# Block 1's feed-forwards: seven block products instead of eight for each pair of up slices, with one weight sum of four made by an accumulating DMA

## What is computed

```python
for l in range(DEPTH):                       # DEPTH = 2
    h = _swiglu(x, ffn_w1[l, 0], ffn_w3[l, 0], ffn_w2[l, 0])
    x = _layernorm(ALPHA * x + 0.5 * h, ln_g[l, 0], ln_b[l, 0])
    h = _mixer(x, l, ...)
    x = _layernorm(ALPHA * x + h, ln_g[l, 1], ln_b[l, 1])
    h = _swiglu(x, ffn_w1[l, 1], ffn_w3[l, 1], ffn_w2[l, 1])
    x = _layernorm(ALPHA * x + 0.5 * h, ln_g[l, 2], ln_b[l, 2])
```

## Time and profile before

| | us |
|---|---|
| median of 3 runs | 1950.27 (1950.02 to 1951.34) |
| the profiled execution's own time | 1950.56 |
| its span | 1948.7 |
| granted TensorE clock, mean | 0.999 |
| TensorE busy | 1919.6 |
| VectorE busy | 1196.0 |
| ScalarE busy | 924.4 |

### The profile page before, as it was taken

How to read it: one execution, slowest core, us unless ns; L and a number is a source line. 1 busy time by engine, 2 the same in 40 slices (tenths; PEclk the granted TensorE clock), 3 DMA queues, 4 the chain that set the end, 5 groups by cost and what they waited for, 6 DMA issues and landing times.

```text
span 1948.7 us, 24336 instructions
## 1 busy us (share of the span) xinstructions
PE 1919.6 (99%) x9160; PEld 1576.5 (81%) x9160; DVE 1196.0 (61%) x1471; ACT 924.4 (47%) x1147; POOL 101.2 (5%) x168
## 2 busy tenths in 40 slices
PE   9999999999999999999999999989999999999999
PEld 7888888888888788888888888877788887778887
DVE  5555866677445645577667655578755466775545
ACT  5443445545443543443554534357644355654443
POOL 2000100000000100010000000011000000100000
PEclk9999999999999999999999999999999999999999
DMA  9675554546655765565354765465365545346542
GB/s 318 196 226 194 200 191 148 173 152 194 215 189 177 219 227 194 173 224 186 131 172 151 225 206 179 148 173 184 128 234 172 172 170 186 119 147 215 179 165 87
DMA packets 202155, 357.69 MB, mean 184 GB/s; under 512 B 8048, under 2 KB 101152, under 8 KB 201824
## 3 DMA queue, kind: packets, MB, share of 16 engines
q1 hardware_dynamic: 195856, 334.85, 51.5%
q0 software_dynamic: 6224, 21.82, 3.9%
HBM read 353.49 MB, written 1.05 MB: 182 GB/s over the span
## 4 chain that ended last, share of the span: by engine, by line
PE 92%; DVE 5%; DVEq 1%; ACT 1%; issue 0%; DMA 0%; SPq 0%
PE acc L717 52%; PE aux L717 32%; DVE w_low L2160 2%; PE aux L833 2%; PE aux L732 1%; PE aux L987 1%; DVE xT_low L2166 0%; DVE x_res L2248 0%; DMA w_raw<-ffn_w 0%; PE aux L997 0%; PE aux L1033 0%; PE aux L996 0%; PE aux L1011 0%; DVE buf_k L2945 0%; DVE x_res L2241 0%
## 5 line engine op out<-in xcount | busy, mean ns | idle before, releaser
L2160 DVE TENSOR_TENSOR w_low<-w_raw,w_high 128x2048 fp32r<-128x2048 f32 (+1 forms) x304 | 686.6, 2271 | 417.3 <-ACT w_high L1589 415.1
L1589 ACT CAST w_high<-w_raw 128x2048 fp32r<-128x2048 f32 (+1 forms) x312 | 586.7, 1896 | 432.3 <-PE acc L717 324.6
L717 PE MATMUL aux<-w_high,xT_high 128*128 128x512 f32 x960 | 380.6, 396 | 3.7 <-DVE xT_low L2166 1.7
L717 PE MATMUL aux<-w_high,xT_low 128*128 128x512 f32 x960 | 374.6, 390 | 0.0
L717 PE MATMUL aux<-w_low,xT_high 128*128 128x512 f32 x960 | 373.9, 389 | 0.0
L717 PE MATMUL acc<-w_high,yT_high 128*128 128x512 f32 (+1 forms) x836 | 329.5, 394 | 0.4 <-issue 0.4
L717 PE MATMUL acc<-w_high,yT_low 128*128 128x512 f32 (+1 forms) x836 | 325.3, 389 | 0.0
L717 PE MATMUL acc<-w_low,yT_high 128*128 128x512 f32 (+1 forms) x836 | 324.8, 388 | 0.0
L717 PE MATMUL acc<-w_high,xT_high 128*128 128x512 f32 (+2 forms) x752 | 297.6, 396 | 5.2 <-DVE xT_low L2166 4.1
L717 PE MATMUL acc<-w_high,xT_low 128*128 128x512 f32 (+2 forms) x752 | 291.3, 387 | 0.0
L717 PE MATMUL acc<-w_low,xT_high 128*128 128x512 f32 (+2 forms) x752 | 291.1, 387 | 0.0
(11 more groups left out here) (343 smaller groups left out, 1351.5 us busy)
## 6 DMA issues: line engine op xcount, KB each, us to landing
w_raw<-ffn_w SPq DMA_DIRECT2D x174, 512.0 KB
w_raw<-w_ff SPq DMA_DIRECT2D x64, 1024.0 KB
w_raw<-w_in SPq DMA_DIRECT2D x52, 1024.0 KB
w_raw<-ffn_w SPq DMA_DIRECT2D x44, 1024.0 KB
w_raw<-w_branch SPq DMA_DIRECT2D x16, 1024.0 KB
w_raw<-o_w_in SPq DMA_DIRECT2D x12, 1024.0 KB
w_raw<-w_ple_gate SPq DMA_DIRECT2D x8, 1024.0 KB
w_raw<-e_w_in SPq DMA_DIRECT2D x6, 1024.0 KB
```

Of the source, the lines that this page charges most:

```text
L717: last = nc.tensor.matmul(dst, lhs[:, kt, tok], rhs(j), start=(kt == k_first and q == 0), stop=(kt == k_last and q == 2))
L1589: nc.scalar.copy(whi[:, s, 0:size], raw[:, s, 0:size]).then_inc(slot_hi[s], 1)
L2160: V.tensor_tensor(wlo[:, s, 0:size], raw[:, s, 0:size], cast(whi[:, s, 0:size]), ALU.subtract)\
```

## The change

Of the 11 slices, 0, 1, 4, 7 and 10 stay as they were ("plain"). The others form three pairs, slices 3q+2 and 3q+3 for q = 0, 1, 2. A pair's up product is X (tiles x halves of k) times W (halves of k x [w1 | w3], 512 columns each), a 2 x 2 product of blocks, done with seven block products instead of eight:

- Four raw blocks are loaded into `buf_v`, `buf_q`, `buf_u` and `buf_val`: R11 and R21 (w1, upper and lower half of k), R12 and R22 (w3).
- VectorE adds in place: R11 + R12, then + R22, then + R21. An accumulating DMA on POOL's queue adds R22 to R12. Products b11, b21, v, x, w, y, b22 use R11, R21, the three sums in R11, the sum in R12, and R22. Each is split into high and low in the ring of slots, so a pair has seven high and seven low halves where its two slices had four of each.
- Four combinations of x (`form`) are made by VectorE once for each feed-forward and split into high and low.
- Terms are copied out of PSUM by ScalarE between products (`term1` to `term3`) and combined by VectorE.

A round is a pair and the plain slice 3q+4. A unit's place in the ring now comes from a table (`ffn_units`). The last slice's down unit has no accumulating DMA any more. The halved first unit of slice 1 goes, as do the halved units at the end; the position angles move to the start of the first feed-forward; the loops over slices are written out. The diff, cut to its core:

```diff
+QUADS = 3
+PLAIN = (0, 1, 4, 7, 10)
+FORMS = 4
...
+def quad_and_plain(q, a, b):
+    o = 3 * q + 4
+    units = [(f"b11_{q}", a), (f"b21_{q}", b), (f"v_{q}", 1), (f"x_{q}", 2), (f"d{o - 3}", a), (f"w_{q}", b),
+ (f"y_{q}", 1), (f"b22_{q}", 2), (f"h{o}_0", b), (f"h{o}_1", a), (f"d{o - 2}", 1), (f"d{o - 1}", 2)]
+    done = [f"b11_{q}", f"b21_{q}", f"v_{q}", f"x_{q}", f"w_{q}", f"d{o - 3}", f"y_{q}", f"b22_{q}",
+f"h{o}_0", f"d{o - 2}", f"d{o - 1}"]
+    return units, done
...
+def quad_load(l, which, q, r):
+    freed = {R11: "y", R21: "y", R12: "w", R22: "b22"}[r]
+    if q > 0:
+        s, n = ffn_unit(l, which, f"{freed}_{q - 1}")
+        sp.wait_ge(slot_lo[s], n + 2)
+    elif which == 1:
+        sp.wait_ge(small_free, l + 1)
+    elif l > 0:
+        sp.wait_ge(quad_free, 2 * l)
+    w = a["ffn_w1" if r in (R11, R21) else "ffn_w3"]
+    r0 = (l * 2 + which) * D + (4 * P if r in (R21, R22) else 0)
+    sp.dma_start(sum_raw[r].rearrange("p (k n) -> p k n", k=4),
+                 rows(w, r0, 4 * P, (3 * q + 2) * FB, 2 * FB)).then_inc(r_full[r], 16)
...
+    hidden1(l, which, 1, 0)
+    hidden1(l, which, 1, 1)
+    quad_load(l, which, 0, R11)
+    down1(l, which, 0)
+    for r in (R12, R21, R22):
+        quad_load(l, which, 0, r)
+    for q in range(QUADS):
+        o = 3 * q + 4
+        down1(l, which, o - 3)
+        hidden1(l, which, o, 0)
+        down1(l, which, o - 2)
+        down1(l, which, o - 1)
+        hidden1(l, which, o, 1)
+        if q + 1 < QUADS:
+            for r in (R12, R21, R11, R22):
+                quad_load(l, which, q + 1, r)
+    down1(l, which, NF - 1)
...
-def last_down_low(l, which):
-    n = 2 * l + which
-    src = raw[:, 3, :]
-    if which == 1:
-        src = rows(a["ffn_w2"], n * F1 + (NF - 1) * FB, FB, 0, D)
-    dst = wlo[:, 3, :] if which == 0 else wlo[:, 3, :].rearrange("p (k n) -> p k n", k=2)
-    pool.wait_ge(last_neg, n + 1)
-    pool.dma_start(dst, src, accum_op=ALU.add).then_inc(last_sum, 16)
-    pool.wait_ge(last_sum, 16 * n + 16)
-    pool.sem_inc(slot_lo[3], 1)
+def sums_by_dma(l, which):
+    for q in range(QUADS):
+        n = quads_before(l, which, q)
+        pool.wait_ge(sum_done, 3 * n + 1)
+        pool.wait_ge(r_full[R22], 16 * n + 16)
+        pool.dma_start(sum_raw[R12], sum_raw[R22], accum_op=ALU.add).then_inc(w_sum, 16)
...
+    def quad_product(name, q, b, lh, ll, first):
+        s = lo_wait(f"{name}_{q}")
+        for k in range(4):
+            for n, (lhs, rhs) in enumerate(((lh, whi), (lh, wlo), (ll, whi))):
+                last = nc.tensor.matmul(aux[:, b, :], lhs(k), rhs[:, s, k * NC:(k + 1) * NC],
+                                        start=(first and k == 0 and n == 0), stop=(k == 3 and n == 2), skip_group_check=not first)
+        last.then_inc(unit_used, 1)
...
+    def quad1(q):
+        o = 3 * q + 4
+        terms, combined = 5 * quads_before(l, which, q), 3 * quads_before(l, which, q)
+        pe.wait_ge(aux_read[1], aux0[1] + q + 3)
+        quad_product("b11", q, 1, *x_part(0, 0), True)
+        pe.wait_ge(aux_read[0], aux0[0] + q + 3)
+        quad_product("b21", q, 0, *x_part(0, 1), True)
+        pe.wait_ge(aux_read[3], aux0[3] + q + 1)
+        quad_product("v", q, 3, *form(0), True)
+        pe.wait_ge(quad_act, terms + 1)
+        quad_product("x", q, 1, *form(1), False)
+        plain_down(o - 3, 0)
+        pe.wait_ge(quad_act, terms + 2)
+        quad_product("w", q, 1, *form(2), False)
+        plain_down(o - 3, 1).then_inc(unit_used, 1)
+        pe.wait_ge(quad_act, terms + 3)
+        quad_product("y", q, 1, *x_part(1, 1), False)
+        pe.wait_ge(quad_read, combined + 2)
+        quad_product("b22", q, 3, *form(3), False)
...
+    hidden_unit(0, 0, 0)
+    hidden_unit(0, 0, 1, mid=lambda: x_T(l, 2 * which, 1, [0]))
+    x_T(l, 2 * which, 1, [1])
+    aux0[2:] = [n_aux[2].k, n_aux[3].k]
+    hidden(0, 1)
+    for j in range(2):
+        hidden_unit(1, 0, j)
+        if j == 1:
+            plain_T(0)
+        hidden_unit(1, 1, j)
+    for p in range(2):
+        pe.wait_ge(acc_read[p], n_acc[p].k + 1)
+    plain_down(0, 0)
+    plain_down(0, 1).then_inc(unit_used, 1)
+    plain_T(1)
+    for q in range(QUADS):
+        o = 3 * q + 4
+        quad1(q)
+        if q + 1 == QUADS:
+            break
+        hidden(o, 0)
+        quad_T(q)
+        hidden(o, 1)
+        for t in range(NT):
+            last = quad_down(o - 2, t)
+        last.then_inc(unit_used, 1)
+        plain_T(o)
+        for t in range(NT):
+            last = quad_down(o - 1, t)
+        last.then_inc(unit_used, 1)
+    i = NF - 1
+    hidden(i, 0)
+    quad_T(QUADS - 1)
+    hidden_unit(i, 1, 0)
+    quad_down(i - 2, 0)
+    quad_down(i - 1, 0)
+    last_T(0)
+    pe.wait_ge(aux_read[2], aux0[2] + FFN_AUX[2] + 1)
+    down_part(i, 0).then_inc(acc_full[0], 1)
+    hidden_unit(i, 1, 1)
+    quad_down(i - 2, 1).then_inc(unit_used, 1)
+    quad_down(i - 1, 1, [0])
...
+    tile1()
+    aux0[2:] = [n_aux[2].k, n_aux[3].k]
+    activate(0, 0)
+    high_plain("h1_0")
+    high_plain("d0")
+    activate(0, 1)
+    high_plain("h1_1")
+    loaded(0, R11)
+    high_sum("b11", 0, R11)
+    for n in range(FORMS):
+        act.wait_ge(form_done, FORMS * (2 * l + which) + (1, 3, 2, 4)[n])
+        nc.scalar.copy(form_h[:, n, :, :].rearrange("p k c -> p (k c)"), quarter[FORM_AT[n]])\
+            .then_inc(form_hi, 1)
+    if mid is not None:
+        mid()
+    used("h1_0")
+    loaded(0, R21)
+    high_sum("b21", 0, R21)
+    activate(1, 0)
+    plain_high_T(0)
+    activate(1, 1)
+    summed(0, 1)
+    high_sum("v", 0, R11)
+    used("d0")
+    plain_high_T(1)
+    summed(0, 2)
+    high_sum("x", 0, R11)
+    for q in range(QUADS):
+        o = 3 * q + 4
+        if q == 0:
+            act.wait_ge(form_lo, FORMS * (2 * l + which) + FORMS)
+        else:
+            act.wait_ge(h_ready, 2 * quads_before(l, which, q))
+        used(f"b11_{q}")
+        nc.scalar.copy(term1, aux[:, 1, :]).then_inc(quad_act, 1)
+        high_plain(f"d{o - 3}")
+        used(f"b21_{q}")
+        act.wait_ge(w_sum, 16 * quads_before(l, which, q) + 16)
+        high_sum("w", q, R12)
+        summed(q, 3)
+        used(f"v_{q}")
+        high_sum("y", q, R11)
+        used(f"x_{q}")
+        nc.scalar.copy(term2, aux[:, 1, :]).then_inc(quad_act, 1)
+        loaded(q, R22)
+        high_sum("b22", q, R22)
+        used(f"w_{q}")
+        nc.scalar.copy(term3, aux[:, 1, :]).then_inc(quad_act, 1)
+        high_plain(f"h{o}_0")
+        act.wait_ge(quad_read, 3 * quads_before(l, which, q) + 1)
+        nc.scalar.activation(term1, term1, ACT.Silu).then_inc(quad_act, 1)
+        used(f"d{o - 3}")
+        high_plain(f"h{o}_1")
+        used(f"y_{q}")
+        nc.scalar.activation(silu1, aux[:, 1, :], ACT.Silu).then_inc(quad_act, 1)
+        high_plain(f"d{o - 2}")
+        used(f"b22_{q}")
+        high_plain(f"d{o - 1}")
+        activate(o, 0)
+        quad_high_T(q)
+        used(f"h{o}_0")
+        if q + 1 == QUADS:
+            break
+        loaded(q + 1, R11)
+        high_sum("b11", q + 1, R11)
+        activate(o, 1)
+        loaded(q + 1, R21)
+        high_sum("b21", q + 1, R21)
+        used(f"d{o - 2}")
+        summed(q + 1, 1)
+        high_sum("v", q + 1, R11)
+        plain_high_T(o)
+        used(f"d{o - 1}")
+        summed(q + 1, 2)
+        high_sum("x", q + 1, R11)
+    high_plain("d10")
...
+    tile1()
+    dve.drain()
+    h0 = n_hi.k
+    whole(1, 0, 0)
+    whole(1, 1, 1)
+    multiply(0, 0)
+    whole(0, 0, 2)
+    low_plain("h1_0")
+    whole(0, 1, 3)
+    dve.drain()
+    combine(1, 0, 1, ALU.subtract)
+    dve.drain()
+    combine(0, 2, 0, ALU.subtract)
+    multiply(0, 1)
+    combine(2, 1, 2, ALU.subtract)
+    dve.drain()
+    combine(3, 3, 2, ALU.add)
+    low_plain("h1_1")
+    low_plain("d0")
+    low_sum("b11", 0, R11)
+    for n in range(FORMS):
+        form_low(n)
+    if mid is not None:
+        mid()
+    add_to(0, R11, R12)
+    low_sum("b21", 0, R21)
+    dve.wait_ge(aux_full[2], n_aux[2].k + 1)
+    multiply(1, 0)
+    plain_low_T(0)
+    multiply(1, 1)
+    for q in range(QUADS):
+        o = 3 * q + 4
+        combined, terms = 3 * quads_before(l, which, q), 5 * quads_before(l, which, q)
+        low_sum("v", q, R11)
+        plain_low_T(1 if q == 0 else o - 3)
+        add_to(q, R11, R22)
+        low_sum("x", q, R11)
+        low_plain(f"d{o - 3}")
+        add_to(q, R11, R21)
+        low_sum("w", q, R12)
+        low_sum("y", q, R11)
+        low_sum("b22", q, R22)
+        dve.wait_ge(quad_act, terms + 1)
+        dve.wait_ge(unit_used, ffn_done(l, which, f"b21_{q}"))
+        V.tensor_tensor(term1, aux[:, 0, :], term1, ALU.add).then_inc(quad_read, 1)
+        dve.wait_ge(quad_act, terms + 3)
+        V.tensor_tensor(term3, aux[:, 3, :], term3, ALU.subtract).then_inc(quad_read, 1)
+        low_plain(f"h{o}_0")
+        low_plain(f"h{o}_1")
+        dve.wait_ge(quad_act, terms + 5)
+        dve.wait_ge(quad_read, combined + 2)
```

(91 more changed lines are left out.)

431 lines of the change are left out of this document (240 added, 191 removed).

## The result

The changed kernel takes 1981.64 us (median of 4 runs, 1981.46 to 1983.09), the kernel before beside it 1950.44: a ratio of 1.016, with an interval of 1.014 to 1.018. It is 31 us slower where 24 were forecast. The profiled execution of the changed kernel took 1983.09 us with a span of 1981.1, 32.4 more than the span of before.

A forecast was written before the change was run, and what follows sets the result against it. TensorE's matmuls were taken to bound the kernel. Net of 32.7 us saved, feed-forwards (9.0 + 2.1 + 2.1 + 1.4), handovers (3.0 + 0.8) and clock (5.6) added 23.9 to 1950.56; by the median 1974 us, range 1958 to 1992.

The forecast's parts named there:

- What goes: Up products of the pairs in four feed-forwards: one block product of 12 matmuls fewer per pair, 32.7 us less.
- Costs by durations: Operation times taken from trace rows; a weight sum in place on VectorE taken as 2.29 us, bounds 2.2 and 2.5.
- Rounds two and three: Later pair rounds of each feed-forward: 47.7 us each on TensorE without a wait, 1.0 us to spare at w.
- Rival 2: Rounds stall too: accumulating DMA taking 18 us costs 2.6 in each later round, giving 1995; slower handoffs 1978; chance 0.12.
- The first down slice: Feed-forward start: TensorE waits for the low half of slice 0's transposed activations, 6.3 us, 11.0 in the first.
- Small terms: Shorter TensorE stalls: slice 1's units 1.1 and 0.4, w of the first pair 1.4, the end 1.1, handovers 1.5 twice and 0.8.
- the end: Last down slice: tile 0's last transposes are followed at once by the product that needs them, 1.1 us per feed-forward.
- the clock: Behind the long stall of each feed-forward the granted clock falls to half: 4 x 1.4 = 5.6 us, bounds 0 and twice the row.
- Rival 1: The clock does not fall in the stalls at the feed-forwards' starts: 1969 us; chance 0.13.
- the first load: First feed-forward: first down slice lands at 26.0 behind as many bytes as before; its later high half costs 2.3 us.
- Rival 3: The feed-forward start does not hold TensorE up: 1939 us; chance 0.08, with what lies between it and no change.
- Rival 4: Whole kernel: the matmuls fall away and the stalls about equal them, 1950 us; chance 0.05.

The follow-up runs named there:

- experiment 7: Changed kernel with the sum R12 + R22 made by VectorE right after low x instead of by the accumulating DMA: 2001.38 us, ratio 1.0265.
- Experiment 6: Changed kernel with three small reorderings (second-term copy ahead of high y, last transposes earlier, slot 1's low half split at handovers): 1975.49 us, ratio 1.0126.
- Experiment 5: Changed kernel with the load of slice 0's down unit issued ahead of raw block R11: 1979.11 us, ratio 1.0148.
- experiment 1: Changed kernel with VectorE's multiply and low half of slice 0's transposes right after low b11, ahead of the combined x: 1958.72 us, ratio 1.0043.
- eighth kernel: Changed kernel with transposes' low half earlier, position angles later, down load before R11, three small reorderings, two form halves in VectorE's gap: 1940.21 us, ratio 0.9943.
- ninth kernel: The eighth kernel plus high b21 after the second activation, low w before the third sum, slice 1's first unit split in halves: 1930.57 us, ratio 0.9897.

## Why the prediction was right, and where it was off

- **What goes**: 144 instructions fewer, 12 in each of 12 pairs. Held.
- **Costs by durations**: a sum in place took 2285 ns (predicted 2.29).
- **Rounds two and three**: no long wait; from the transposes of slice 4 to those of slice 7 in the second feed-forward 47.6 us (552.08 to 599.69), predicted 47.7. The count to w with 1.0 to spare stood at 1.2 in experiment 7. Rival 2 fell.
- **The first down slice**, the largest term: 6.3 predicted in each of three feed-forwards, 6.12, 6.08 and 6.11 measured. The low half begins 24.0 us behind the start of tile 1 of slice 0, predicted 23.9 (458.11 to 482.0). In the first, 11.0 predicted and 8.57 measured; TensorE had been held up 3 us more before it, and by the slow clock, and so arrived later.
- **Small terms**: first unit of slice 1 1.1, measured 1.1 (in the third feed-forward 0.55); second unit 0.4, measured 0.26; w 1.4, measured 1.1; the end 1.1, measured 0.9; first handover to a mixer 1.5, measured 1.25; the other one 1.5, measured 1.0; from the second to the third feed-forward 0.8, measured 1.0. Experiment 6 bears out the end. It bears out about half of the handovers, and w had two late inputs.
- **Mis-sized: the clock.** The step "nine products of 384 columns ... so 1.4 us were lost. A stall of 6.3 us should do that each time: 4 x 1.4" took one sample as the price. The runs show 1.5 to 2.9, and five such stalls, not four: 12.9 in place of 5.6. Rival 1, that the clock does not fall, fell as well; the bound "twice the row" (2.8) was the better value.
- **Put at nothing: what a wait costs beyond its row.** The sum took each stall at its length. By the chain a wait costs 0.3 more. The second feed-forward bears that out: it lost 6.0 us, where 10.0 of waits in the rows and 2.9 of slow clock against 8.2 saved give 4.7, so 1.3 is left for four waits more. Up to block 2 the changed kernel has 18 waits more than the kernel before: by this estimate some 5 us.
- **Mis-sized: the first load.** The step from "behind as many bytes as before" to a landing at 26.0 failed. The bytes are as many, but not their times: before, the extra unit ahead of it (the last slice's) was issued at 5.30, and now R11 is issued at 15.66, 0.55 us ahead of it. Experiment 5 put 5.9 us on that. ScalarE could begin at 30.0, and TensorE waited 5.52 where 2.3 were counted. The raw blocks behind it seem to cost it little: in experiment 5 all four stand there, and it lands at 24.1, sooner than before the change.
- **Together**: by the handovers, the four feed-forwards cost 17.0, 6.0, 5.8 and 3.2, where 11.9, 4.3, 5.0 and 2.8 were forecast (24.0, which the sum has as 23.9). The first alone holds 5.1 of the 8 us by which the sum is short. The clock (7.3), the waits beyond their rows (5) and the first load (3.2) were too small by more than that; that the sum came as near is luck in part, since the first feed-forward's down slice (2.4) and most small terms were counted too large.
- **Rival 3**, the start without a stall, fell as a statement on this kernel, but its condition can be made true: with the transposes' low half moved forward (experiment 1) and the rest put in order, the kernel is faster than before. The 1939 that it gave is near the eighth kernel's 1940 by chance: that kernel still had one stall of 6.13, and had lost other waits in return. Rival 2's 2.6 us does not follow from its own bound either: 18 us against 14 would be 4. Rival 4, no change, fell.

## What to carry to other kernels

Where fewer matmuls are bought with more work on the engines that prepare their operands, count each engine's program order up to every operand, not its busy share: here 71% busy cost 31 us in one order, and 73% gained 20 in another. Put ahead in an in-order queue what TensorE needs next, and behind it whatever may wait for a load. After mending a wait look for the second input that is nearly as late, and price a stall of TensorE above its own length, here by 0.3 us for every wait and by 1.5 to 2.9 more where the clock falls. When two variants differ by less than such a stretch, compare them stage by stage.

## What was not expected of the hardware

For equal stalls the number of slow products varied: fourteen behind 6.12 and 6.08 us, seven behind 6.11, seven or eight behind 3.72, none behind 1.53 at the down slice. The windows tell what differs. In the second feed-forward the clock was still full for 5.3 us of the stall and low from 499.2 to 506.0; in the fourth it was low from 1137.5 to 1144.3. Both times that is 6.8 us, but in the fourth 3.9 us of it lay in the idle time, where it costs nothing. (In the first row 0.60 is the mean of a microsecond whose last 0.8 is low.)

```profile
499.00:500.00 1.00, 0.00 (x0) 0.60 1.31 262
...
1137.60:1141.30 3.70, 0.00 (x0) 0.50 0.80 218
1141.40:1144.20 2.80, 2.80 (x7) 0.50 1.03 211
```

Why it fell early in one stall and late in the other, and why some waits of 1.2 to 2.3 us at the handovers brought it down and others did not, was not settled.

The accumulating DMA of 1 MB within SBUF took 7.0 us as the median of twelve in the changed kernel. The slower ones were the first of the third feed-forward (10.1) and the first of the first: 7.8 where it was issued at 49.8 us, 11.2 in experiment 5 (issued at 44.0) and 11.3 in the ninth kernel (41.4), the nearer to the start's loads the slower. Whether those loads are the cause was not tried.
